# One TensorE kernel, one core: the modulation's matrix product moved from TensorE to VectorE and to later stages, and three small pieces of attention moved by some steps

## The reference, cut to what matters

```python
def diff_attention_layer(x, ...):            # 16 heads of 128, q and k in two halves of 64
    h = rms_norm(x, norm_g); q, k, v, z = split(h @ w_in)
    q, k = rms_norm(q) * 0.125, rms_norm(k)  # per half
    probs = softmax(q k^T + bias)            # causal, by query block, for both halves
    o = (probs[0] - lam * probs[1]) @ v
    return x + (rms_norm(o) * silu(z)) @ w_out

mod = (silu(c) @ ada_w + ada_b).reshape(B, 3, 3, 1024)       # (1 x 1024) @ (1024 x 9216)
shift, scale, gate = mod[:, :, 0], mod[:, :, 1], mod[:, :, 2]
h = rms_norm(x) * (1 + scale[0]) + shift[0]
x = x + 0.5 * gate[0] * swiglu(h, ffn1_w_in, ffn1_w_out)     # then the mixer with mod 1, ffn2 with mod 2
```

## Time and profile before

| | |
|---|---|
| median of 3 runs | 1898.52 us (1898.12 to 1898.67) |
| span of the profiled execution, first to last instruction | 1896.2 us |
| PE busy | 1868.0 us, 99% |
| DVE, ACT busy | 996.8 us, 817.9 us |
| attention (head 1's first scores to head 15's) | 73.97 to 463.15 us |
| the eight tiles of out0 | 555.7 to 642.9 us |
| feeds by POOL's queue | 42.21 MB |

### The profile page before, as it was taken

How to read it: one execution, slowest core, us unless ns; L and a number is a source line. 1 busy time by engine, 2 the same in 40 slices (tenths; PEclk the granted TensorE clock), 3 DMA queues, 4 the chain that set the end, 5 groups by cost and what they waited for, 6 DMA issues and landing times.

```text
span 1896.2 us, 22387 instructions
## 1 busy us (share of the span) xinstructions
PE 1868.0 (99%) x8923; PEld 1450.5 (76%) x8923; DVE 996.8 (53%) x1778; ACT 817.9 (43%) x1328; POOL 123.8 (7%) x148
## 2 busy tenths in 40 slices
PE   8999999999999999999999999999999999999997
PEld 6566666666788788888886777778888878888886
DVE  6667666666544653333346667845434763333322
ACT  6566656656633342222323655434432442222221
POOL 0111111110001000000010011000000100000000
PEclk9999999999999999999999999999999999999999
DMA  5444343432233232222333323221123323233331
GB/s 199 164 145 156 144 145 145 145 145 101 78 129 117 67 111 100 93 96 94 100 86 125 99 70 106 68 94 35 45 89 111 124 92 102 94 100 97 92 95 61
DMA packets 56526, 201.95 MB, mean 107 GB/s; under 512 B 6478, under 2 KB 6934, under 8 KB 55784
## 3 DMA queue, kind: packets, MB, share of 16 engines
q1 hardware_dynamic: 44616, 158.32, 25.3%
q0 software_dynamic: 11808, 42.21, 6.1%
HBM read 195.23 MB, written 5.28 MB: 106 GB/s over the span
## 4 chain that ended last, share of the span: by engine, by line
PE 87%; DVE 6%; ACT 4%; issue 1%; DMA 0%; SPq 0%; DVEq 0%; ACTq 0%
PE ps L1204 25%; PE ps L1207 24%; PE ps L1205 24%; PE ps L1304 2%; PE ps L1268 2%; PE ps L1340 1%; ACT wH L1910 1%; PE ps L1292 1%; DVE wL L1499 1%; PE ps L1280 1%; ACT a L2009 1%; DVE a L1622 1%; PE ps L1347 1%; PE ps L1257 1%; DVE g1a L1499 1%
## 5 line engine op out<-in xcount | busy, mean ns | idle before, releaser
L1204 PE MATMUL ps<-hH,wH 128*128 128x512 f32 (+1 forms) x1560 | 634.8, 407 | 1.0 <-DVE hL L1570 1.0
L1207 PE MATMUL ps<-hH,wL 128*128 128x512 f32 (+1 forms) x1560 | 610.7, 391 | 1.0 <-DVE wL L1499 0.7
L1205 PE MATMUL ps<-hL,wH 128*128 128x512 f32 (+1 forms) x1560 | 609.0, 390 | 0.0
L1499 DVE TENSOR_TENSOR wL<-wr,wH 128x1024 fp32r<-128x1024 f32 (+2 forms) x285 | 343.9, 1207 | 483.8 <-ACT wH L1910 483.2
L1910 ACT ACTIVATE wH<-wr 128x1024 fp32r<-128x1024 f32 (+2 forms) x285 | 295.1, 1036 | 233.3 <-PE ps L1207 218.3
L1204 PEld LDWEIGHTS ps<-hH,wH 128*128 128x128 f32 (+1 forms) x1560 | 292.7, 188 | 93.6 <-issue 32.4
L1207 PEld LDWEIGHTS ps<-hH,wL 128*128 128x128 f32 (+1 forms) x1560 | 292.3, 187 | 66.9 <-DVE wL L1499 3.9
L1205 PEld LDWEIGHTS ps<-hL,wH 128*128 128x128 f32 (+1 forms) x1560 | 293.1, 188 | 61.3 <-issue 6.5
L1204 PE MATMUL ps<-gffn,wH 128*128 128x512 f32 x400 | 157.0, 393 | 1.0 <-DVE xT L1677 0.9
L1205 PE MATMUL ps<-gffn,wH 128*128 128x512 f32 x400 | 155.8, 390 | 0.0
L1207 PE MATMUL ps<-gffn,wL 128*128 128x512 f32 x400 | 155.8, 390 | 0.0
(11 more groups left out here) (304 smaller groups left out, 2079.9 us busy)
## 6 DMA issues: line engine op xcount, KB each, us to landing
wr<-wst SPq DMA_DIRECT2D x268, 512.0 KB, 3.4
a<-wfd POOLq DMA_DIRECT2D x54, 512.0 KB, 5.0
xT<-wfd POOLq DMA_DIRECT2D x18, 512.0 KB, 6.9
wr<-wst SPq DMA_DIRECT2D x16, 384.0 KB, 3.0
xT<-xin SPq DMA_DIRECT2D x8, 256.0 KB, 6.8
xT<-xin SPq DMA_DIRECT2D x2, 1024.0 KB, 7.0
xsave<-xT SPq DMA_DIRECT2D x1, 2048.0 KB, 7.3
c<-wfd POOLq DMA_DIRECT2D x8, 256.0 KB, 3.7
```

Source lines behind the costliest of these rows:

```text
L1204: e.matmul(o, hi, xh[k], start=k == 0, stop=False)
L1205: e.matmul(o, hi, xl[k], start=False, stop=False)
L1207: i = e.matmul(o, lo, xh[k], start=False, stop=k == t.nk - 1)
L1499: e.tensor_tensor(dst, x, hi.bitcast(F32), ALU.subtract).then_inc(s[name], 1)
```

## The change

- The 18 units `ada` go. In their place VectorE multiplies each 128x1024 block of `ada_w` by its number of `csil` and adds it to a sum (`fed`, one instruction, L1726 or L1729), over the eight blocks of rows. TensorE then adds over the 128 partitions with a column of ones (`fed_sum`, L1335, four or two products). There are five parts: parts 0 and 1 (what ffn1 needs, 24 products) under out0, one each three blocks from step 6 on; parts 2 to 4 (48 products) under ffn1, two a tile from j = 2 on. The feeds move with them; their buffers lie where `hH` and `hL` are free, and where ffn1's last products will stand.
- The modulation is read back and turned in two pieces, `mod` under tile 5 of out0 and `mod2` in ffn1. The `raw` steps of ffn1 move from tiles 4 to 7 to tiles 6 and 7.
- `SCHED`: `vturn` from step 10 to 9, `turnw` from 4, 7, 7, 13 to 7, 7, 9, 14. The ring `mi` is 6, 5, 7.

```diff
-SCHED = {"rstd": 1, "v": 10, "table": 2, "c": [(9, (0, 1)), (14, (2,)), (18, (3,))], "w": [11, 12, 16, 21],
-         "c0": [(14, (0, 1)), (17, (2,)), (20, (3,))], "w0": [16, 17, 19, 22], "d": [4, 7, 7, 13], "pv": 18, "ada": 30,
+SCHED = {"rstd": 1, "v": 9, "table": 2, "c": [(9, (0, 1)), (14, (2,)), (18, (3,))], "w": [11, 12, 16, 21],
+         "c0": [(14, (0, 1)), (17, (2,)), (20, (3,))], "w0": [16, 17, 19, 22], "d": [7, 7, 9, 14], "pv": 18, "ada": 30,
...
+FED = [(0, 2), (2, 1), (3, 2), (5, 2), (7, 2)]
+FED_AT = [8 * sum(n for _, n in FED[:p]) for p in range(len(FED))]
...
+    def fed(self, i, end):
+
+        self.add("fed", i=i, next=i + ADA_BUFS if i + ADA_BUFS < end else None, a2v=self.sig("a2v"))
+
+    def fed_sum(self, p):
+        self.add("fed_sum", p=p, adm=self.sig("adm"), row=self.sig("row"))
+        self.move("fed_row", p=p)
+
+    def fed_later(self, i, k):
+
+        if i < 24 and k == 3:
+            for j in range(2):
+                self.fed(FED_AT[2] + 2 * i + j, len(ADA))
+        if k == 5 and i in (8, 16, 24):
+            self.fed_sum(i // 8 + 1)
+        if k == 1 and i == 27:
+            self.move("fed_mod")
+        if k == 7 and i == 28:
+            self.add("mod2", modt=self.sig("modt"))
...
-        pb, mi, sc = Ring([0, 1]), Ring([6, 5]), Ring([2, 3, 4])
+        pb, mi, sc = Ring([0, 1]), Ring([6, 5, 7]), Ring([2, 3, 4])
...
-            for n in range(NADA):
-                if ada_step(n) // 24 == i:
-                    put(ada_step(n) % 24, ada, n)
...
-        more = {4: [lambda: add("mod_rest"), lambda: self.raw(1, 0), lambda: self.raw(1, 1)],
-                5: [lambda c=c: self.raw(1, c) for c in (2, 3, 4)], 6: [lambda: self.raw(1, 5)], 7: [lambda: self.raw(1, 6)]}
+        more = {7: [lambda: self.raw(1, 6)]}
         at = {(6, 9): lambda: self.shift_row(1, 0, first), (7, 1): lambda: self.shift_row(1, 1, first + 1),
-              (7, 8): lambda: self.shift_row(1, 2, first + 2)}
+              (7, 8): lambda: self.shift_row(1, 2, first + 2), (5, 12): lambda: add("mod", modt=sig("modt")),
+              (5, 4): lambda: self.move("mod_in"), (6, 1): lambda: add("mod_rest")}
+        for step, chunks in ((6, 3), (0, 2)), ((6, 7), (2, 4)), ((6, 12), (4, 5)), ((7, 3), (5, 6)):
+            at[step] = lambda chunks=chunks: [self.raw(1, c) for c in range(*chunks)]
+        add("fed_start", done=self.h_lasts[1], i=0, n=FED_AT[2])
+        fed, sums = {6 + 3 * i: i for i in range(FED_AT[2])}, {}
...
+                if 16 * c + k in fed:
+                    i = fed[16 * c + k]
+                    self.fed(i, FED_AT[2])
+                    if i + 1 in FED_AT:
+                        sums[16 * c + k + 3] = fed_unit(i)[0]
+                if 16 * c + k in sums:
+                    self.fed_sum(sums[16 * c + k])
...
+                elif what == "fed_sum":
+                    p = d["p"]
+                    take(7)
+                    bank_free[7] = ("row", d["row"])
+                    w.wait_ge(s["a2v"], FED_AT[p] + 8 * FED[p][1])
+                    for q in range(2 * FED[p][1]):
+                        acc = fed_views(FED_AT[p] + q // 2)[0]
+                        i = e.matmul(ps[7][32 * q:32 * q + 1, :], C("one", 0, 1), acc[:, 512 * (q % 2):512 * (q % 2) + 512],
+                                     start=True, stop=True)
+                    i.then_inc(s["adm"], 1)
...
+                elif what == "fed":
+                    i = d["i"]
+                    p, k, j = fed_unit(i)
+                    acc, buf = fed_views(i)
+                    w.wait_ge(s_ada[i % ADA_BUFS], 16 * (i // ADA_BUFS + 1))
+                    if k == 0:
+                        if p > 2:
+                            w.wait_ge(s["adm"], p)
+                        e.tensor_scalar(acc, buf, csil[:, 0:1], None, ALU.mult, ALU.bypass).then_inc(s["a2v"], 1)
+                    else:
+                        w.wait_ge(s["a2v"], i + 1 - FED[p][1])
+                        e.scalar_tensor_tensor(acc, buf, csil[:, k:k + 1], acc, ALU.mult, ALU.add).then_inc(s["a2v"], 1)
...
+                elif what == "fed_start":
+                    w.wait_ge(s["slot"], d["done"])
+                    for i in range(d["i"], d["i"] + ADA_BUFS):
+                        fed_feed(i)
+                elif what == "fed":
+                    if d["next"] is not None:
+                        w.wait_ge(s["a2v"], d["a2v"])
+                        fed_feed(d["next"])
```

More of the change, by code:

```diff
@@ L558, in ffn @@
         self.whole(up(1))
+        if sub == 0:
+            add("fed_start", done=self.h_lasts[1] + 16, i=FED_AT[2], n=len(ADA))
         for j in range(2, 22):
-            self.whole(gate(j))
-            self.whole(up(j))
+            for i, t in enumerate((gate(j), up(j))):
+                for k in self.steps_of(t):
+                    if sub == 0:
+                        self.fed_later(2 * (j - 2) + i, k)
         self.h_lasts[n + 1] = len(self.slots)
@@ L977, in model_kernel @@
             F = ExitStack()
-            G = Arena(F, f"gffn{f}", 22 * 1024, F32R)
+            G = Arena(F, f"gffn{f}", (22 - 6 * (f == 0)) * 1024, F32R)
+            if f == 0:
+                with ExitStack() as early:
+                    E = Arena(early, "fed", 6 * 1024)
+                    fed_acc, fed_buf = E.several(2, 1024), E.several(4, 1024)
+                late = Arena(F, "gffn_late", 6 * 1024, F32R)
+                aH, aL = (G.several(16) + late.several(6) for _ in range(2))
+            else:
+                aH, aL = G.several(22), G.several(22)
             A = Arena(F, f"affn{f}", 4992)
-            ff.append(dict(aH=G.several(22), aL=G.several(22), sq=A.several(2), rs=A(), tmp=A.several(2), sg=A.several(2),
+            ff.append(dict(aH=aH, aL=aL, sq=A.several(2), rs=A(), tmp=A.several(2), sg=A.several(2),
                            ac=A.several(2), row=A(384)))
@@ L1018, in model_kernel, with fed_views @@
         g_order = [h for z in range(6) for h in (6 + z, z)] + list(range(12, HEADS))
+        fed_row, mod_row2 = ff[0]["sq"][0], ff[0]["sq"][1][:, 0:128]
+        def fed_views(i):
+            p, _, j = fed_unit(i)
+            return (fed_acc0[2 * p + j], fed_buf0[i % ADA_BUFS]) if p < 2 else (fed_acc[j], fed_buf[i % ADA_BUFS])
         s = {name: ctx.enter_context(nc.semaphore("s_" + name)) for name in plan.count}
-        for name in ("small", "const", "first", "lam", "csil", "hi", "lo", "slot", "th", "rowd", "xb0", "xb1", "modin", "mod", "modd", "saved", "bd", "ba",
+        for name in ("small", "const", "first", "lam", "hi", "lo", "slot", "th", "rowd", "xb0", "xb1", "modin", "mod", "modd", "saved", "bd", "ba",
                      "bp", "crz", "outs", "dv", "ac", "dn2", "ob", "dso", "dsi", "slv", "dsb", "sba"):
@@ L1499, in lo_of, with factors @@
                 e.tensor_tensor(dst, x, hi.bitcast(F32), ALU.subtract).then_inc(s[name], 1)
+            def factors(subs):
+                for sub in subs:
+                    j, a = 24 * sub, gs[:, 8 * sub:8 * sub + 8]
+                    own(e.tensor_scalar(a, mod[:, j + 8:j + 16], 1.0, None, ALU.add, ALU.bypass))
+                    own_done()
+                    e.tensor_tensor(a, a, S("ng", 8 * sub, 8 * sub + 8), ALU.mult)
+                    e.tensor_scalar(gate[:, 8 * sub:8 * sub + 8], mod[:, j + 16:j + 24], 0.5, None,
+                                    ALU.mult, ALU.bypass).then_inc(s["modd"], 1)
+                w.wait_ge(s["modd"], subs[-1] + 1)
             for what, d in steps:
@@ L1679, in _ @@
                     w.wait_ge(s["mod"], 1)
-                    for sub in range(3):
-                        j, a = 24 * sub, gs[:, 8 * sub:8 * sub + 8]
-                        own(e.tensor_scalar(a, mod[:, j + 8:j + 16], 1.0, None, ALU.add, ALU.bypass))
-                        own_done()
-                        e.tensor_tensor(a, a, S("ng", 8 * sub, 8 * sub + 8), ALU.mult)
-                        e.tensor_scalar(gate[:, 8 * sub:8 * sub + 8], mod[:, j + 16:j + 24], 0.5, None,
-                                        ALU.mult, ALU.bypass).then_inc(s["modd"], 1)
-                    w.wait_ge(s["modd"], 3)
+                    factors(range(1))
                 elif what == "out_up":
@@ L2066, in _ @@
                     f, j = ff[d["f"]], d["j"]
+                    if d["f"] == 0 and j == 16:
+                        w.wait_ge(s["adm"], 5)
                     w.wait_ge(s["fu"], d["fu"])
```

104 lines of the change are left out of this document (40 added, 64 removed).

## The result

| | before | after |
|---|---|---|
| median | 1898.53 us (1898.12 to 1898.67) | 1911.34 us (1910.3 to 1912.81) |
| span of the profiled execution | 1896.2 us | 1908.8 us |
| ratio of the medians, 95% interval | | 1.0067 (1.0053 to 1.0082) |

What follows compares the result with a forecast made beforehand. A VectorE and ScalarE chain was taken to bound attention, TensorE out0 and ffn1. Terms -8.4 - 3.3 + 5.3 + 0.2 + 1.2 + 1.1 + 1.9 = -2.0 took the median from 1898.5 to 1896.5 us; 8-in-10 range 1880 to 1912.

Steps and rivals of the forecast that it cites:

- The chain of 27.2 us a head: Attention: a chain through VectorE and ScalarE sets each head at 27.2 us, whatever TensorE does beside it.
- The rival by which TensorE sets attention: Attention: TensorE sets the heads, so 30 us come back (1868), or half of it (1882); chance 0.18, whole or part.
- Part 1: Attention without modulation units: 8.4 us gained from head 1 to 15, 3.3 in the last heads, 0 in the first.
- Part 2: Attention: turned blocks in pairs, v's turn ahead of the first scores and a third bank, costed at nothing.
- Durations: Out0 and ffn1: a VectorE product taken at 1.29 us, a small TensorE sum at 1.05, five sums 5.3.
- The waits at the two sums, 1.2 us: Out0: VectorE ends 0.6 us after TensorE is ready at each of two sums, 1.2 us; above 6 only if transfers lag.
- SP's waits for rows at 0: SP's queue waits for three more rows before sending weights, each wanted over a tile later; cost 0.
- The end of out0, +1.1: Out0's last two tiles: five more products of x by the norm's scale make the last residual add 1.1 us later.
- The clock, 1.9 us: Attention: TensorE's new gap at L1257 may halve its clock in some heads; taken as rare, 1.9 us in all.
- The rival that feeds cannot keep up (1905): Out0: feeds take 2.5 us instead of 2.04, TensorE waits at both sums, 1905 us; chance 0.15 including the ffn1 case.
- the ffn1 case: Ffn1: products hold up the splits and later sums stall TensorE, costing about as much as slow feeds; shared chance 0.15.
- The rival of the clock in most heads (1914): Attention: the clock falls to half in most heads at the new gap, 20 us instead of 1.9, 1914 us; chance 0.25 for many heads.

Runs made afterwards that it cites:

- filler: The kernel after, with 8 products of the old unit's shape added on TensorE ahead of the second tile (step 8) of heads 1 to 15; 1921.79 us, ratio 1.0118.
- old_steps: The kernel after, with the table of small steps of the kernel before (v's turn at 10, turned blocks at 4, 7, 7, 13); 1910.22 us, ratio 1.0065.
- row_later: The kernel after, with SP's transfer of part 0's row two weight slots later in its queue; 1910.20 us, ratio 1.0062.

## Why the prediction was wrong, by its own steps

- **The chain of 27.2 us a head**: right. 27.15 us measured, 2.05 us of waiting at L1291, and 27 us of added work that vanished in it. The rival by which TensorE sets attention is out. "Whatever TensorE has to do beside it" was too wide (filler). The rival's half gain should have read 1883.5, not 1882; nothing hangs on it.
- **Part 1**: -8.4 and -3.3 forecast, -9.2 and -3.7 measured (the first is -7.7 with the 1.5 us of the one head whose clock fell). Right. The first head lost 0.6 us where I had 0, within what the starts of different executions differ by (the first weight product of attention's tiles stands between 40.0 and 42.2 us in these runs).
- **Part 2 at nothing**: right for the moved steps (old_steps). The third bank by itself was not tested.
- **Durations**: a product took 1279 ns in ffn1 and 1369 in out0 (1.29 taken); a sum's eight instructions 0.98 us from start to start and about 0.2 at their two ends, about 1.2 (1.05 taken, three of them 3.5 where I had 3.2).
- **The waits at the two sums, 1.2 us**: this step failed. TensorE waited 5.6 us there, and about 2 more were lost at half clock behind the first. The first sum alone began 8.7 us behind a TensorE that waits for nothing (46.3 against 37.6). Its part "at out0's start 2 MB of x come back at the same time, so feeds 4 to 8 come 2 us late, and catch up before product 15. Taken at 0" was wrong three times over. I counted the feeds as late and not the weights, which share the DMA engines with them and stand in SP's queue behind x; I did not ask what VectorE has queued behind the split of a late weight (its products); and I let it catch up, although the rows left it little room for that: a tile of 10.9 us wants 5.3 products, two splits and an add, 5.3 x 1.2 + 2 x 1.14 + 0.6 = 9.3 us by starts, so it regains 1.6 us a tile, and it owed six products and a split, over 8 us. The forecast itself named the case, "above 6 only if the transfers lag", and I took the other end. "Long waits before the new sums (L1335)" stood among its signs of being wrong, and came.
- **The late weights themselves**, 1.8 us of waiting at TensorE and a clock that fell behind them (0.50 from 565 to 568 us), had no step at all. At TensorE itself they cost little, since VectorE sets when the sum can start, and what TensorE loses ahead of it shortens its wait there. In filler TensorE waited 0.8 us for weights and 6.5 at the first sum, against 1.8 and 4.7, and out0 took the same 104.5 us.
- **SP's waits for rows at 0**: right (row_later), although SP stood 21.2 us at the first one.
- **The end of out0, +1.1**: right in kind (the residual add behind `raw` and shift rows), too small: 2.7 - 0.85 = 1.85 us, and then 1.6 us in ffn1's first tiles, which began at half clock and had no step.
- **The clock, 1.9 us**: by its place in attention right, one head of 14 and 1.5 us. That was luck in part: the figure was picked between two rows that said opposite things. Outside attention the clock cost about 2 us behind the first sum, 1.6 at ffn1's start and 1.5 in the mixer, whose gap I had counted among those that keep the clock.

Out0 alone carries 11.9 us more than I had, the clock behind it 3.1, ffn1 0.6. Attention is 1.6 us better than my sum, with the 0.6 of the start against it: 11.9 + 3.1 + 0.6 - 1.6 + 0.6 = 14.6, from -2.0 to +12.6. The rival that feeds cannot keep up (1905) came nearest in its mechanism. It too had only the wait at the sums, and 0.15 for it and the ffn1 case together was too little, with 353 of 410 GB/s in my own working before the 2 MB of x were added. The rival of the clock in most heads (1914) is nearer in its number by luck: the clock fell in one head of 14.

The prediction cited the Trainium skill, page "SBUF — State Buffer", section "Who interferes with whom", for GpSimd's hold on VectorE's instructions with two SBUF inputs. Here the three products in the row at 582.01 (4.71 us) took 1.04 us more than those in the row at 567.20 (3.67); GpSimd's addition ran from 581.79 for 1.45 us, and the first product, which has two SBUF inputs, started in it:

```profile
581.79 1.45 POOL L2290 TENSOR_TENSOR b<-b 128x512 f32<-128x512 f32 x1
```

The trace agrees for that one, and it cost VectorE about one microsecond a tile while it was the bound. The 1.32 us row, which the prediction took as agreeing, is a TENSOR_SCALAR with one tensor input (`b<-wr,tiny`): it shows a delay of the same 1.04 us (0.28 without one), but not the case of two inputs.

## What to carry to other kernels

Work taken from the busiest engine is worth what the stage's own chain lets through: measure a free place with fillers before moving the work elsewhere, since here the same units, moved by a few steps, cost nothing. When a stream of transfers is added, list what else shares the DMA engines in its first 10 to 20 us, and what is queued in order behind the instruction that waits for the latest of them; a weight that comes late holds everything behind its split. A reduction that waits for a whole stream belongs as late as its consumer allows, and its slack is counted from the stream's own rate. And where one engine sets when a later step can start, the waits that another has on the way there are not added to the last one: with less of the first, the last only grew (filler).
